# A two-layer transformer trunk on one core: a fifteenth ring slot, and five pieces of work moved on TensorE and VectorE

## The chip, the cores and the metric

The kernel runs on one core of a Trainium2 chip. What is measured is the device time of one execution in microseconds (us); the median over several runs counts.

## What is computed

One sequence of 256 tokens of width 1024 passes two layers, all in float32. Layer 0 mixes tokens with forgetting attention, layer 1 with sparse attention; each is followed by a mixture of 64 experts.

```
for layer in range(2):
    sh_m, sc_m, g_m, sh_f, sc_f, g_f = split(silu(c) @ w_ada[layer] + b_ada[layer], 6)
    u = rmsnorm(h) * (1 + sc_m) + sh_m
    mix = forgetting_attention(u) if layer == 0 else nsa_attention(u, shared_kv(h))
    h = h + g_m * mix
    u = rmsnorm(h) * (1 + sc_f) + sh_f
    h = h + g_f * moe_ffn(u)
# nsa_attention: o = gate0 * o_compressed + gate1 * o_selected + gate2 * o_window
#   o_compressed: softmax of each head's queries over 4 compressed keys, times 4 compressed values
# moe_ffn: s = sigmoid(u @ w_router); the top 8 of 64 by s + bias, weights s / sum * 2.5
#   y = sum over the 8 of weight * (silu(u @ w_eg) * (u @ w_eu)) @ w_ed, plus one shared expert
```

## The kernel before

**The ring.** All large weights pass through `ring` in SBUF, in units of 1 MB. `RING` lists the 484 units in the order in which they are loaded and used; unit n goes to slot n % SLOTS, with SLOTS = 14. The SyncE queue (SP) issues them one after the other (`unit`, `slot_free`): before unit n it waits until TensorE has finished with unit n - SLOTS. There is no other order: if that unit is still held, every later load waits behind it.

**The experts.** In each layer the 64 experts are ordered by how many tokens chose them and cut into 25 groups (`GROUPS`) of one, two or four experts whose rows fill the 128 partitions. An expert has three units: two halves of its gate and up weights, and its down weights. Groups 0 and 1 hold four fixed experts, so that their 12 units can be loaded ahead of the routing. From group 2 on SP must read the order (`order_i`), which routing makes. In `pe_moe` group g runs on TensorE (PE) as: gate and up product (`pe_gate_up`, two halves), gather of the next group's tokens (`pe_gather`, two halves of 8 matmuls), `pe_turn`, the combination of group g - 1 (`combine`), down product (`pe_down`). ScalarE (ACT) copies each gathered half from PSUM (`copy_x`, signalled by `x_ready`). In groups 0 and 1 both halves of a gather are written to the one bank GATHER, so that the second half waits until the first has been copied. `item_tables` makes two small tables in bank Y0 + 1 for experts with more rows than their place holds; before the down product of group 0, which writes that bank, PE waits for `tables_ready`, which VectorE (DVE) gives once it has read them.

**Routing.** At the start of `pe_moe` PE turns the normed rows (`pe_turn_normed`, token tile 0, then tile 1), multiplies by the router weights (`pe_narrow`), turns u back (16 transposes), turns the scores into rows, and then spreads the gate vector over the partitions (`pe_gate`, two matmuls of 128x512 over `gate_diag`, which DVE makes in `dve_gate_diag`). DVE picks the top 8 after it has the scores.

**Sparse attention.** Sixteen batches of four heads (`attention_batches`): 0 to 3 and 8 to 11 are of token tile 0 (128 keys), 4 to 7 and 12 to 15 of tile 1 (256 keys). In step b of `pe_attention` PE makes logits b + 2, weighs values for b - 1 (`weigh`) and turns the probabilities of b (`turn`). In step b of `dve_attention` DVE runs `beside(b)`, masks b + 2 (`mask`) and scales the output of b - 1 (`output`). In step b of `act_attention` ACT takes the exponentials of b and then copies the turned probabilities of b - 1, which `weigh(b - 1)` waits for. Two pieces of DVE work stand beside: at b = 0 the copy of the gates out of bank 6 and `cmp_scores`; at b = 3 `cmp_weights`, five instructions, whose result PE needs first in `weigh(6)` (`CMP_TURNED_AT` is 6).

```
            for b in range(len(batches)):
                if beside:
                    beside(b)
                if b + 2 < len(batches):
                    mask(b + 2)
                if b >= 1:
                    output(b - 1)
```

`add_mix` on DVE then adds the attention's product to h in three pieces of 256 columns, and the last quarter per token tile, each followed by `dve_row_norm`.

## Time and profile before

| | |
|---|---|
| time, median of 3 runs | 1437.22 us (1435.86 to 1437.52) |
| the profiled execution | 1438.07 us, of which the span from first to last instruction is 1436.3 us |
| PE busy | 1381.5 us, 96% of the span |
| DVE, ACT busy | 321.2 us, 266.1 us |
| moved from HBM | 509.89 MB, 356 GB/s over the span |
| share of PE in the chain that ended last | 89% |
| expert groups of layer 0, of layer 1 | about 255 to 731 us, about 953 to 1429 us |

Times in the rows are in us from the start of the span. A matmul's end is modelled, so that a busy PE is not a PE at its peak. A row's bracket gives the idle time of the engine before it and what ended it. PEclk is the clock that TensorE was granted, as a share of 2.4 GHz.

### The profile page before, as it was taken

What the parts mean: (1) busy time and instruction counts of PE and PEld (TensorE: products, weight loads), DVE (VectorE), ACT (ScalarE), POOL (GpSimd) and SP (SyncE); (2) the same over time, 40 slices, a digit from 0 to 9 for tenths busy, and PEclk for the clock granted to TensorE, in tenths of its full rate; (3) what the DMA queues carried; (4) which work ended last, traced back from release to release, by engine and by line L of the source; (5) the groups of instructions that cost most, each with busy time, mean ns of one, the idle gap of its engine ahead of it and who ended that gap; (6) DMA issues with size and microseconds to landing.
All of it is one profiled execution on the core that took longest, in us unless ns stands there. A gap on an engine that the chain in (4) does not pass through costs nothing.

```text
span 1436.3 us, 20547 instructions
## 1 busy us (share of the span) xinstructions
PE 1381.5 (96%) x8361; PEld 788.8 (55%) x8361; DVE 321.2 (22%) x776; ACT 266.1 (19%) x519; POOL 31.6 (2%) x79
## 2 busy tenths in 40 slices
PE   5999899999999999999989988999999999999997
PEld 1777765555644444444458867854564444444442
DVE  1330523111111111111133477231110111111111
ACT  2211523110101111111133365231101111111110
POOL 5000000000100000000000000000010000000000
PEclk9999999999999999999999989999999999999999
DMA  9999289899999999999998600148999999999997
GB/s 376 413 421 421 115 338 407 351 389 420 364 420 421 420 421 420 421 422 420 420 418 332 233 30 1 61 174 363 421 374 404 421 420 421 420 420 421 421 420 289
DMA packets 71599, 512.30 MB, mean 357 GB/s; under 512 B 8240, under 2 KB 8432, under 8 KB 9552
## 3 DMA queue, kind: packets, MB, share of 16 engines
q1 hardware_dynamic: 70560, 509.64, 86.4%
q0 software_dynamic: 800, 1.25, 0.3%
q8 instruction: 68, 1.11, 0.3%
q14 instruction: 27, 0.22, 0.0%
q10 hardware_dynamic: 144, 0.08, 0.0%
HBM read 509.89 MB, written 1.05 MB: 356 GB/s over the span
## 4 chain that ended last, share of the span: by engine, by line
PE 89%; DMA 5%; DVE 3%; ACT 2%; issue 1%; SPq 0%; DVEq 0%; ACTq 0%
PE PS L925 23%; PE PS L915 13%; PE PS L933 12%; PE PS L536 12%; PE PS L949 11%; DMA ring<-in_w_exp 4%; PE PS L563 3%; PE PS L683 2%; PE PS L961 2%; DMA ring<-in_w_ada_units 1%; PE PS L1797 1%; PE PS L515 1%; PE PS L547 1%; PE PS L970 1%; PE PS L666 1%
## 5 line engine op out<-in xcount | busy, mean ns | idle before, releaser
L925 PE MATMUL PS<-ring,scratch 128*32 128x512 f32 (+2 forms) x2176 | 355.4, 597 | 7.3 <-DMA ring<-in_w_exp 5.9
L925 PEld LDWEIGHTS PS<-ring,scratch 128*32 128x32 f32 (+2 forms) x2176 | 111.5, 123 | 244.2 <-issue 242.3
L915 PEld LDWEIGHTS PS<-scratch,u 128*128 128x128 f32 x1600 | 183.0, 192 | 38.7 <-issue 36.8
L915 PE MATMUL PS<-scratch,u 128*128 128x128 f32 x1600 | 192.5, 278 | 1.4 <-ACT scratch L1149 1.4
L933 PE MATMUL PS<-ring,scratch 128*32 128x512 f32 (+2 forms) x1088 | 182.2, 596 | 2.3 <-DVE item_first_i L1265 1.2
L949 PE MATMUL PS<-scratch 128*128 128x512 f32 x384 | 172.7, 592 | 0.0
L1285 DVE TENSOR_TENSOR scratch<-PS,gate_row 128x512 f32<-128x512 f32 x100 | 69.2, 692 | 461.5 <-PE PS L933 461.5
L536 PE MATMUL PS<-ring,uT 128*128 128x256 f32 x672 | 149.3, 381 | 0.4 <-ACT uT L494 0.4
L1157 ACT ACTIVATE scratch<-PS 128x256 f32<-128x256 f32 x50 | 19.2, 384 | 675.2 <-PE PS L925 675.2
L536 PEld LDWEIGHTS PS<-ring,uT 128*128 128x128 f32 x672 | 126.1, 190 | 23.0 <-issue 6.5
L933 PEld LDWEIGHTS PS<-ring,scratch 128*32 128x32 f32 (+2 forms) x1088 | 52.6, 122 | 122.3 <-issue 120.6
L949 PEld LDWEIGHTS PS<-scratch 128*128 128x128 f32 x384 | 69.2, 190 | 68.9 <-issue 68.9
L1273 DVE TENSOR_TENSOR scratch<-scratch,PS 128x256 f32<-128x256 f32 x50 | 21.1, 422 | 331.6 <-ACT scratch L1157 331.6
L1149 ACT ACTIVATE scratch<-PS 128x512 f32<-128x512 f32 x100 | 59.7, 597 | 142.8 <-PE PS L915 142.8
L563 PE MATMUL PS<-ring,cond_cols 128*32 128x512 f32 x448 | 56.5, 626 | 14.3 <-DMA ring<-in_w_ada_units 14.3
L683 PE MATMUL PS<-scratch,uT 128*128 128x65 f32 x288 | 39.2, 289 | 9.7 <-ACT uT L713 9.4
L683 PEld LDWEIGHTS PS<-scratch,uT 128*128 128x128 f32 x288 | 35.9, 201 | 17.0 <-ACT uT L713 15.0
L721 ACT ACTIVATE scratch<-scratch,stats 128x128 f32<-128x128 f32 (+1 forms) x96 | 35.6, 443 | 15.2 <-DVE stats L742 15.2
L563 PEld LDWEIGHTS PS<-ring,cond_cols 128*32 128x32 f32 x448 | 12.1, 111 | 46.5 <-issue 32.4
L1162 ACT ACTIVATE scratch<-PS 128x512 f32<-128x512 f32 x50 | 29.6, 592 | 2.7 <-PE PS L943 2.7
L536 PE MATMUL PS<-ring,u 128*128 128x256 f32 x128 | 28.7, 381 | 0.0
L961 PE MATMUL PS<-uT,ring 128*128 128x256 f32 x128 | 28.3, 379 | 0.0
(332 smaller groups left out, 851.2 us busy)
## 6 DMA issues: line engine op xcount, KB each, us to landing
ring<-in_w_exp SPq DMA_DIRECT2D x384, 1024.0 KB, 16.6
ring<-in_w_ada_units SPq DMA_DIRECT2D x56, 1024.0 KB, 17.0
ring<-in_w_in_a_units SPq DMA_DIRECT2D x12, 1024.0 KB, 26.1
ring<-in_w_cmp_units SPq DMA_DIRECT2D x8, 1024.0 KB, 26.2
ring<-in_w_sh_units SPq DMA_DIRECT2D x6, 1024.0 KB, 13.6
ring<-in_w_kv_b_units SPq DMA_DIRECT2D x6, 1024.0 KB, 22.4
ring<-in_w_o_a_units SPq DMA_DIRECT2D x4, 1024.0 KB, 10.8
ring<-in_w_in_b_units SPq DMA_DIRECT2D x4, 1024.0 KB, 11.3
```

Of the source, the lines that this page charges most:

```text
L536: mm = pe_.matmul(PS[:, bank, t * UC:(t + 1) * UC], lhs[:, k, t * P:(t + 1) * P], w[:, k, :], start=(k == 0), stop=(k == KC - 1))
L563: mm = pe_.matmul(PS[32 * k:32 * k + 32, ADA, :], cond_cols[:, j % 2 * (KC // 2) + k, 31 - r:63 - r], w[:, k, :], start=(j == ada_units(st ...
L683: mm = pe_.matmul(PS[:, heads_bank(kind, b), hd * (DH + 1):(hd + 1) * (DH + 1)], pT[:, n * P:(n + 1) * P], values(br, kt, 4 * g + hd), sta ...
L721: eng.activation(p, p, ACT.Exp, bias=stats[:, b % 3, 4 + i:5 + i]).then_inc(probs_ready, 1)
L915: mm = pe_.matmul(PS[:, bank, i * w:(i + 1) * w], u[:, t, k * P:(k + 1) * P], hot[:, t, :], start=(t == 0), stop=(t == NT - 1))
L925: mm = pe_.matmul(PS[places, GU, :], x[:, kk, places], gate_and_up, start=(kk == 0), stop=(kk == KC - 1))
L933: mm = pe_.matmul(PS[places, Y0 + half, :], hT[:, j, places], down[:, j, half * 512:(half + 1) * 512], start=(j == 0), stop=(j == 1))
L949: mm = pe_.matmul(OUT[t][:, half * 512:(half + 1) * 512], hot_wT[0:rows, t * P:(t + 1) * P], y_rows[0:rows, half * 512:(half + 1) * 512], ...
L961: mm = pe_.matmul(PS[:, GATHER, i * SEQ:(i + 1) * SEQ], slot(AT[unit])[:, k, i * P:(i + 1) * P], uT[:, k, :], start=(k == 0), stop=(k == K ...
L1149: act.activation(x_pair[g % 2][:, 4 * half:4 * half + 4, :].rearrange("p k s -> p (k s)"), PS[:, gather_bank(g, half), :], ACT.Copy).then_ ...
L1162: act.activation(turned_sb[g % 2], PS[:, GU, :], ACT.Copy).then_inc(group_sem["turned_copied"], 1)
L1285: dve.tensor_tensor(y_rows[:, half * 512:(half + 1) * 512], PS[:, Y0 + half, :], gate_row[:, half * 512:(half + 1) * 512], ALU.mult).then_ ...
```

## The change

It has five parts. **Ring:** SLOTS is 15. **Gathers:** the second half of the gather for group 0 goes to bank GU and that for group 1 to bank 0, and PE no longer waits there for the first half's copy; `end_ps` and the item tables move to bank 2, and the wait for `tables_ready` moves from ahead of group 0's down product to ahead of the first `combine` in group 1. **Gates:** DVE copies the gates right after `rotate(3)`, ahead of the first mask, and not after the second. **Compressed weights:** `cmp_weights` runs at b = 6 and not at b = 3. **Last gate:** in layer 1 `gate_diag` is made within `add_mix`, after the second piece; one of its two matmuls stands between the turns of the two token tiles, the other after u has been turned back; and the scores are turned between the two tiles of turning u back.

```
-SLOTS = 14
+SLOTS = 15
...
+        def pe_gate_half(pe_, i, half):
+            return pe_.matmul(PS[:, 4 * (i % 2) + half, :], ones[:, :],
+                              gate_diag[:, 4 * half:4 * half + 4, :].rearrange("p k c -> p (k c)"),
+                              start=True, stop=True)
...
-        def pe_turn_normed(pe_, tag):
+        def pe_turn_normed(pe_, tag, beside_norm=None):
             for t in range(NT):
+                if t == 1 and beside_norm:
+                    beside_norm()
...
-        end_ps = PS[E64, Y0 + 1, 0:1]
+        end_ps = PS[E64, 2, 0:1]
...
         def gather_bank(g, half):
-            return Y0 + 1 if half and g > 1 else GATHER
+            return [GU, 0][g] if half and g <= 1 else Y0 + 1 if half else GATHER
...
-            pe_turn_normed(pe_, tag)
+            def first_of_gate():
+                pe_.wait_ge(gate_diag_ready, 4)
+                pe_.wait_ge(mix_added, 5 * layer + 2)
+                pe_gate_half(pe_, 3, 1)
+
+            pe_turn_normed(pe_, tag, first_of_gate if layer else None)
...
+            turn_back(0)
+            if layer == 0:
+                turn_back(1).then_inc(routing["u_turned"], 1)
             pe_.wait_ge(routing["sigmoids"], layer + 1)
             pe_narrow_rows(pe_, narrow_T[E64, :], scores_ps).then_inc(routing["scores_ready"], 1)
-            pe_gate(pe_, 2 * layer + 1)
+            if layer == 0:
+                pe_gate(pe_, 1)
+            else:
+                turn_back(1).then_inc(routing["u_turned"], 1)
+                pe_gate_half(pe_, 3, 0).then_inc(gate_out, 1)
...
-            pe_.wait_ge(*by_group("x_ready", layer, 1))
-            pe_gather(pe_, one_hot[0], range(4, 8)).then_inc(group_sem["gathered"], 1)
+            pe_gather(pe_, one_hot[0], range(4, 8), gather_bank(0, 1)).then_inc(group_sem["gathered"], 1)
...
                     if g:
                         pe_.wait_ge(*by_group("y_ready", layer, 2 * g))
-                    else:
-                        pe_.wait_ge(*by_group("x_ready", layer, 3))
...
                 if g:
+                    if g == 1:
+                        pe_.wait_ge(routing["tables_ready"], layer + 1)
                     combine(g - 1)
                 else:
                     item_tables()
-                    pe_.wait_ge(routing["tables_ready"], layer + 1)
...
-            dve_gate_diag(done, 2 * layer + 1)
+            if layer == 0:
+                dve_gate_diag(done, 1)
...
+                    if (layer, j) == (1, 1):
+                        dve.wait_ge(gate_out, 3)
+                        dve_gate_diag(done, 3)
...
             rotate(3)
+            dve.wait_ge(sem("gates_turned"), 1)
+            done(dve.tensor_copy(gates[:, :, :], narrow_rows(6, SEQ, 3 * H)), sem("gates_ready"))
...
                 if b == 0:
-                    dve.wait_ge(sem("gates_turned"), 1)
-                    done(dve.tensor_copy(gates[:, :, :], narrow_rows(6, SEQ, 3 * H)), sem("gates_ready"))
                     cmp_scores()
-                elif b == 3:
+                elif b == CMP_TURNED_AT:
                     cmp_weights()
```

On PE, where layer 1's expert part begins, before the change (L547 is the last quarter of the attention's output product, L827 the turn of the normed rows, L515 the router product, L994 turning u back, L523 turning the scores, L605 the gate):

```order
L547 MATMUL PS<-ring,uT 128x256 x16
L827 MATMUL PS<-ident,u 128x128 x16
L515 MATMUL PS<-uT,scratch 64x256 x8
L994 MATMUL PS<-ident,uT 128x128 x16
L523 MATMUL PS<-ident,narrow_T 128x64 x2
L605 MATMUL PS<-scratch,ones 128x512 x2
L1003 MATMUL PS<-scratch,before 128x64
```

The same place after the change (L831, L1006 and L608 are the former L827, L994 and L605):

```order
L547 MATMUL PS<-ring,uT 128x256 x16
L831 MATMUL PS<-ident,u 128x128 x8
L608 MATMUL PS<-scratch,ones 128x512
L831 MATMUL PS<-ident,u 128x128 x8
L515 MATMUL PS<-uT,scratch 64x256 x8
L1006 MATMUL PS<-ident,uT 128x128 x8
L523 MATMUL PS<-ident,narrow_T 128x64 x2
L1006 MATMUL PS<-ident,uT 128x128 x8
L608 MATMUL PS<-scratch,ones 128x512
L1023 MATMUL PS<-scratch,before 128x64
```

One gate matmul has moved between the two turns, and 8 transposes from ahead of the scores to behind them.

On DVE, in the sparse attention before the change, between output 1 (L2215) and mask 5 (L738, L741, L742) stand the five instructions of `cmp_weights`:

```order
L2215 TENSOR_TENSOR u<-PS,stats 128x256
L2191 TENSOR_REDUCE small<-scratch 128x32
L2192 RECIPROCAL small<-small 128x32
L2193 TENSOR_TENSOR small<-small,gates 128x32
L2195 TENSOR_TENSOR scratch<-scratch 128x128
L2196 TENSOR_TENSOR scratch<-scratch,small 128x128
L738 TENSOR_TENSOR scratch<-PS,causal 128x1024
```

After the change they stand between output 4 (L2237) and mask 8 (L740), the first of the second branch:

```order
L2237 TENSOR_TENSOR u<-PS,stats 128x256
L2215 TENSOR_REDUCE small<-scratch 128x32
L2216 RECIPROCAL small<-small 128x32
L2217 TENSOR_TENSOR small<-small,gates 128x32
L2219 TENSOR_TENSOR scratch<-scratch 128x128
L2220 TENSOR_TENSOR scratch<-scratch,small 128x128
L740 TENSOR_TENSOR scratch<-PS,causal 128x512
```

So three masks of 256 keys (5, 6 and 7) now run ahead of them, and the mask behind them is one of 128 keys.

On DVE in `add_mix` of layer 1 after the change (L841, L843 are a piece's product and sum, L2102, L2104 those of the last quarter), `gate_diag` (L597) has moved from behind the modulation to between the second and the third piece:

```order
L841 TENSOR_TENSOR scratch<-PS,gate_row 128x512
L843 TENSOR_TENSOR h<-h,scratch 128x2x256
L597 TENSOR_TENSOR scratch<-ident,vectors 128x1024
L841 TENSOR_TENSOR scratch<-PS,gate_row 128x512
L843 TENSOR_TENSOR h<-h,scratch 128x2x256
L2102 TENSOR_TENSOR scratch<-PS,gate_row 128x256
L2104 TENSOR_TENSOR h<-h,scratch 128x256
```

## Rows read from the trace of the kernel before

**Rows 1.** Busy time by stretch, most of each layer's expert groups; last columns PEclk, DMA, GB/s.

```profile
390.00:714.00 324.00, 323.82 (x1936) 152.16 (x1934) 43.60 (x90) 35.13 (x68) 0.00 (x0) 1.00 1.01 421
1090.00:1412.00 322.00, 321.78 (x1931) 151.35 (x1929) 43.61 (x90) 35.13 (x68) 0.00 (x0) 1.00 1.01 421
```

**Rows 2.** PE's waits over the whole span: total, times, longest.

```profile
PE PS L925 <- DMA ring<-in_w_exp: 5.9, 2, 3.2
```

**Rows 3.** PE's timeline, last group of layer 0: second gate/up half, down product.

```profile
716.59 5.34 PE L925 MATMUL PS<-ring,scratch 128*32 128x512 f32 x32 [2.77 <-DMA ring<-in_w_exp]
...
727.04 2.35 PE L933 MATMUL PS<-ring,scratch 128*32 128x512 f32 x20
```

**Rows 4.** The same of layer 1.

```profile
1414.94 3.64 PE L925 MATMUL PS<-ring,scratch 128*32 128x512 f32 x32 [3.17 <-DMA ring<-in_w_exp]
...
1424.85 3.64 PE L933 MATMUL PS<-ring,scratch 128*32 128x512 f32 x32 [1.09 <-DMA ring<-in_w_exp]
```

**Rows 5.** The chain that ended last: start, length of its two long transfers.

```profile
692.85 23.61 DMA ring<-in_w_exp
...
1397.81 26.90 DMA ring<-in_w_exp
```

**Rows 6.** What the DMA engines moved from 1066 to 1086 us, slices of 0.5 us.

```profile
GB/s 442 410 410 475 377 426 426 164 98 66 49 0 147 98 197 426 377 492 328 262 66 213 328 475 426 360 164 147 164 344 442 475 328 377 262 328 410 459 328 410
```

**Rows 7.** Timelines of PE and ACT, layer 0, end of group 0.

```profile
265.38 2.05 PE L915 MATMUL PS<-scratch,u 128*128 128x128 f32 x16 [0.69 <-ACT scratch L1149]
...
268.80 3.65 PE L933 MATMUL PS<-ring,scratch 128*64 128x512 f32 x16 [0.62 <-DVE item_first_i L1265]
...
267.96 0.59 ACT L1162 ACTIVATE scratch<-PS 128x512 f32<-128x512 f32 x1
```

**Rows 8.** Timelines in the sparse attention, batches 3 to 6: DVE, ACT, PE.

```profile
847.08 0.29 DVE L2191 TENSOR_REDUCE small<-scratch 128x32 f32<-128x128 f32 x1
...
848.35 0.29 DVE L2196 TENSOR_TENSOR scratch<-scratch,small 128x128 f32<-128x128 f32 x1
...
851.40 1.71 ACT L721 ACTIVATE scratch<-scratch,stats 128x256 f32<-128x256 f32 x4 [3.01 <-DVE stats L742]
...
854.06 3.67 PE L683 MATMUL PS<-scratch,uT 128*128 128x65 f32 x16 [2.57 <-ACT uT L713]
...
860.55 2.00 PE L683 MATMUL PS<-scratch,uT 128*128 128x65 f32 x16
...
864.55 2.00 PE L683 MATMUL PS<-scratch,uT 128*128 128x65 f32 x16 [0.47 <-ACT uT L713]
```

**Rows 9.** Busy time by stretch: PE, weight loads, DVE, ACT, POOL; PEclk third last.

```profile
848.64:872.05 23.41, 19.76 (x152) 17.55 (x151) 17.68 (x39) 12.13 (x27) 0.00 (x0) 0.85 0.01 1
935.00:939.00 4.00, 3.97 (x11) 2.24 (x12) 2.32 (x4) 2.35 (x4) 0.00 (x0) 0.57 0.00 0
853.50:860.50 7.00, 6.39 (x32) 5.87 (x32) 5.55 (x11) 3.24 (x7) 0.00 (x0) 0.52 0.00 0
```

**Rows 10.** Timelines of PE and ACT where the gates are awaited.

```profile
836.42 1.05 PE L1744 MATMUL PS<-own_group,ada_parts 128*128 128x32 f32 x8 [1.32 <-DVE gates L2202]
...
835.57 0.58 ACT L1953 ACTIVATE ada_parts<-PS 128x512 f32<-128x512 f32 x1
```

**Rows 11.** PE's timeline into layer 1's routing; then the router product of layer 0.

```profile
933.59 1.09 PE L827 MATMUL PS<-ident,u 128*128 128x128 f32 x8 [1.82 <-DVE u L818]
935.03 5.35 PE L515 MATMUL PS<-uT,scratch 128*64 128x256 f32 x16 [0.35 <-DMA scratch<-in_w_router_rows]
940.32 1.97 PE L994 MATMUL PS<-ident,uT 128*128 128x128 f32 x16
...
237.91 3.64 PE L515 MATMUL PS<-uT,scratch 128*64 128x256 f32 x16 [0.15 <-ACT uT L494]
```

**Rows 12.** DVE's timeline there: third piece of the mix, and the gate's diagonal.

```profile
924.10 0.69 DVE L837 TENSOR_TENSOR scratch<-PS,gate_row 128x512 f32<-128x512 f32 x1 [2.94 <-PE PS L1797]
...
936.11 1.22 DVE L597 TENSOR_TENSOR scratch<-ident,vectors 128x1024 f32<-128x1024 f32 x1
```

More of the change, by code:

```diff
@@ L603, in pe_gate @@
             pe_.wait_ge(gate_diag_ready, i + 1)
-            for half in range(2):
-                mm = pe_.matmul(PS[:, 4 * (i % 2) + half, :], ones[:, :],
-                                gate_diag[:, 4 * half:4 * half + 4, :].rearrange("p k c -> p (k c)"),
-                                start=True, stop=True)
-            mm.then_inc(gate_out, 1)
+            pe_gate_half(pe_, i, 0)
+            pe_gate_half(pe_, i, 1).then_inc(gate_out, 1)
+        def pe_gate_half(pe_, i, half):
+            return pe_.matmul(PS[:, 4 * (i % 2) + half, :], ones[:, :],
+                              gate_diag[:, 4 * half:4 * half + 4, :].rearrange("p k c -> p (k c)"),
+                              start=True, stop=True)
         def act_gate(done, i):
@@ L899, in build @@
         count_ranked_ps = PS[E64, Y0, 320:321]
-        end_ps = PS[E64, Y0 + 1, 0:1]
-        n_items_ps = PS[0:1, Y0 + 1, 1:2]
-        item_rank_ps = PS[0:1, Y0 + 1, 128:128 + MAX_ITEMS]
-        item_base_ps = PS[0:1, Y0 + 1, 192:192 + MAX_ITEMS]
+        end_ps = PS[E64, 2, 0:1]
+        n_items_ps = PS[0:1, 2, 1:2]
+        item_rank_ps = PS[0:1, 2, 128:128 + MAX_ITEMS]
+        item_base_ps = PS[0:1, 2, 192:192 + MAX_ITEMS]
         count_col, rank_col, key_e, n_over, end_col, begin_col, base_col = (e_cols[E64, i:i + 1] for i in range(7))
         def gather_bank(g, half):
-            return Y0 + 1 if half and g > 1 else GATHER
+            return [GU, 0][g] if half and g <= 1 else Y0 + 1 if half else GATHER
         def pe_gather(pe_, hot, chunks, bank=GATHER):
@@ L989, in pe_moe, with turn_back @@
                 pe_ada_columns(pe_, 2)
-            for t in range(NT):
+            def turn_back(t):
                 for k in range(KC):
@@ L995, in pe_moe @@
                                        uT[:, k, t * P:(t + 1) * P], ident[:, :])
-            mm.then_inc(routing["u_turned"], 1)
+                return mm
+            turn_back(0)
+            if layer == 0:
+                turn_back(1).then_inc(routing["u_turned"], 1)
             pe_.wait_ge(routing["sigmoids"], layer + 1)
             pe_narrow_rows(pe_, narrow_T[E64, :], scores_ps).then_inc(routing["scores_ready"], 1)
-            pe_gate(pe_, 2 * layer + 1)
+            if layer == 0:
[3 more added lines that the diff above has]
+                pe_gate_half(pe_, 3, 0).then_inc(gate_out, 1)
             pe_.wait_ge(routing["mask_ready"], layer + 1)
```

## The prediction

> **What bounds the kernel now.** I read the busy time by stretch first, then PE's waits, then the timelines where it waits. Through most of the expert groups both bounds are at work at once: PE is busy without a gap and the DMA engines move 421 GB/s [rows 1]. One unit is 1.049 MB, so it takes 2.49 us at that rate. PE hardly waits for weights: twice, 5.9 us together [rows 2], and both waits stand in the last group of a layer [rows 3, 4]. So PE sets the pace from group 0 on, the loads lose a little ground to it, and at the end of each layer the loads have become the bound. The chain that ended last shows the same: it goes through PE and then through one transfer, from 692.85 to 716.46 in layer 0 and from 1397.81 to 1424.71 in layer 1 [rows 5]. Those transfers are long because they stand in a full queue, not because they are slow.
>
> What ties the loads' end is the last time at which the ring was full and the DMA engines stood idle. That is at about 1069.5 to 1080 us: the rate falls from above 400 to between 0 and 200 GB/s three times [rows 6], since SP may issue only as PE frees a slot. Behind it the rate is 421 GB/s to the end [rows 1]. So each layer's loads end at that event, which PE times, plus the number of units still to come.
>
> Ahead of the experts of layer 1 PE waits for DVE and ACT instead: in the attention [rows 8, 10] and at the router [rows 11]. An idle spell there can cost twice, as the granted clock falls behind it: 0.52 from 853.5 to 860.5 and 0.57 from 935 to 939 [rows 9], the lower of the two levels (1.2 GHz) for nearly all of the stretch.
>
> **The change part by part.**
>
> *Ring.* With 15 slots SP is one unit further when the ring is last full, and all behind it come 2.49 us earlier, in each layer. In layer 1 PE waits 3.17 us for the second gate/up half and 1.09 us for the down weights [rows 4]. Both waits depend on loads that come 2.49 us earlier, and PE's own work between them is unchanged, so 0.68 us is left of the first and the second stays: **2.49 us** gained. In layer 0 more is to be had. PE's second half starts at 716.59 after 2.77 us, and takes 5.34 us, where the same 32 matmuls took 3.64 in layer 1 [rows 3, 4]: the clock had fallen behind the wait. With 0.28 us of it left I take the full clock. In layer 1 PE was ready for the down product 8.82 us after that half's start (1424.85 - 1.09 - 1414.94) [rows 4]; in layer 0 that would be 714.10 + 8.82 = 722.9. The last down unit landed at 716.46 + 4 x 2.49 = 726.4 [rows 5] and now lands at 723.9, so the loads decide, and the down product starts at 724.0 in place of 727.04 [rows 3]: **3.0 us**. If PE has slack nowhere else, this needs no other change. Its bounds are 0 (the loads don't get ahead) and the whole waits, 2.77 + 1.7 and 3.17 + 1.09.
>
> *Gathers and tables.* In group 0, PE waited 0.69 us between the halves of the gather and 0.62 us for the tables [rows 7]. The first wait goes whole: nothing else is behind it. The second doesn't: ACT's copy of what `pe_turn` made ended at 268.55 [rows 7], 0.25 us before the down product started, and PE needs that copy too. It moves with the gather, so I take 0.69 + 0.2 = **0.9 us in each layer**, 1.8 in all; 1.4 without the second part, 2.6 if both waits went whole. Both move PE, and as PE times the last full ring, the loads come as much earlier. Moving the tables' wait ahead of `combine` costs nothing: a down product and a whole gate/up product of work (3.65 us for the first alone [rows 7]) lie between. The same change for group 0's own gather costs and gives nothing, since small products stand between its halves. The wait for the last copy of group 0's tokens stays.
>
> *Gates.* PE waited 1.32 us, and the row names DVE's gates [rows 10]. But the same matmuls also read `ada_parts`, whose copy by ACT ended at 836.15 [rows 10], only 0.27 before. So 0.1 us, 0.3 at most. On DVE the copy stands in another place with the same length ahead of the second mask's end.
>
> *Compressed weights.* The five instructions run from 847.08 to 848.64, 1.6 us [rows 8]. Behind them comes mask 5, then the exponentials of batch 5 at 851.40 (ACT had waited 3.01 us for them), and only behind these ACT's copy for `weigh(4)`, which PE reaches at 854.06 after 2.57 us [rows 8]. With the five away, and the 0.1 from above, `weigh(4)` starts 1.7 us earlier, at 852.4, and 0.9 us of the wait is left. Then there is the clock. From this `weigh` to the next PE took 6.49 us (854.06 to 860.55), at 0.52 of the clock; the next such step, at full clock, took 4.00 [rows 8, 9]. With 0.9 us of idle time in place of 2.57, I take the clock as kept: 2.49 us more. Sum **4.2 us**. DVE must be able to follow. From 848.64 to 872.05, where it begins to be the bound again, it was busy for 17.68 of 23.41 us in 39 instructions [rows 9]; each is followed by a pause of 0.03 us (848.64 to 848.68 behind the last of the five is one), 1.2 in all, so 4.5 us was waiting. Adding the moved 1.6, it needs 20.5 where 25.0 went by: it can come 4.5 earlier, and so follows the 4.2. The result is needed in `weigh(6)`, at 852.4 + 2 x 4.0 = 860.4; the five end on DVE once mask 7 and output 4 are done, about 859.3, by the order of its work. If the clock falls all the same, 1.7 us remains; if DVE merely waits elsewhere, 0.
>
> *Last gate.* Making the diagonal takes 1.22 us and now stands ahead of the third piece, where DVE sat idle for 2.94 us [rows 12]: no cost; without that cover it would be 1.2. One gate matmul of 512 columns fills part of the 1.82 us before the second turn. Its length is at least 0.5 us, a quarter of the 2048 columns that were turned in 1.97 us [rows 11], and I take twice that, as a product of two full f32 operands should cost more per column than a turn; at either end it fits into the wait and delays nothing. What it may give is the clock: the router product took 5.35 us in layer 1 and 3.64 in layer 0, where PE was busy until it [rows 11], so **1.7 us**, or 0. Turning back half of u behind the scores takes half of 1.97 us [rows 11] off the way to DVE's top 8: 0.95 us. From there DVE's chain leads to the first gather without waiting; ACT's copy of u ends as late as before, and its gate copy comes 0.1 to 0.2 earlier, just not in the way. I take **0.9 us**, 0.5 if ACT comes last.
>
> **The clock's rule.** The trace shows two drops behind waits of 1.82 and 2.57 us [rows 9, 8, 11], and none behind the longest, 3.17 us, since the product behind it took 3.64 us [rows 4]. The Trainium skill, "TensorE: Matmul & The Clock Gate", Part 1, explains it: the window in which activity is judged runs freely, and the place of a drop can vary with the phase. By that, shifting the program may take a drop away here and set one there. The trace agrees as far as a long wait without a drop goes; the rule gives weight to rival 1.
>
> **Sum.** 2.49 + 3.0 + 1.8 + 4.2 + 1.7 + 0.9 = 14.1 us. Span 1436.3 - 14.1 = 1422.2; the profiled run of 1438.07 becomes 1424.0, and the median of 1437.22, 0.85 less than that run, **1423.1 us**.
>
> **Rivals.**
> 1. *The clock falls elsewhere or still* (one or two of: batch 4, the router, or a place that kept it so far). Each costs 1.7 to 2.5 us (5.35 - 3.64; 6.49 - 4.00) [rows 8, 11]. For it: idle spells stay at every one of these places, and the whole of layer 1 is shifted. Against: the spells are a half to a third as long. 1425 to 1428 us.
> 2. *The wait moves within the attention.* DVE has but 0.3 us to spare over PE, and mask 8 now stands behind the five instructions. If they only delay it instead of mask 5, 4.2 shrinks to 1.7 or nothing: 1425.6 to 1427.3 us. Against: 4.5 us of waiting in that stretch [rows 9].
> 3. *The ring's slot gives nothing*, as if the queue of issued transfers and not the slots held the loads back, or PE were slower by another wait: 14.1 - 5.5 = 8.6, 1428.6 us. Against it are the idle DMA engines [rows 6].
> 4. *Slower than before.* Each transfer behind the last full ring takes longer, because the deeper ring is served less evenly. About 130 units per layer follow (324 / 2.49) [rows 1]. An interval longer by 14.1 / 260 = 0.054 us, 2.2%, takes everything back, and at 4% the time is 1436 + 12 = 1449 us. Nothing in the trace bears on it: the rate is 421 GB/s however full the queue is [rows 1].
>
> **Chances and range.** The forecast (1421.3 to 1424.9) 0.53; rival 1 0.27; rival 2 0.07; rival 3 0.07; rival 4 0.02; better than forecast, if a drop that I left in place goes too, 0.04. The range reaches from 1420.8 to 1428.2. A measurement of this kernel can tell about 0.2%, 2.9 us, from no change; only rival 4 and a pile of the others fall short of that. Faster 0.96, same 0.02, slower 0.02.
>
> **What would show it.** *Ring:* the wait at the last group's second half falls to about 0.3 us in layer 0 and 0.7 in layer 1; that in front of the last down product stays near 1.1 us. *Group 0:* the waits of 0.69 and 0.62 us are replaced by one of some 0.4 us. *Attention:* a wait of about 0.9 us before `weigh(4)`, PEclk 1.00 behind it, and 4.2 us less between mask 4 and mask 11. *Router:* the product takes 3.6 us, and the wait ahead of the second turn is 0.8 to 1.3 us. Wrong would be: PEclk near 0.5 in a new place (rival 1), no wait left in a layer's last group while the layer is not 2.5 us shorter (PE is the bound, rival 3), or a rate below 421 GB/s (rival 4).

## The result and the profile after

The kernel after takes 1433.12 us (median of 20 runs, 1428.43 to 1438.13) beside 1438.34 us of the kernel before in the same series (20 runs, 1435.52 to 1450.51): a ratio of 0.9944, 95% interval 0.9925 to 0.9962. It is faster, by 5 us where 14 were forecast, and lies above the range. The profiled execution took 1437.93 us, its span is 1436.2 us, and its mean granted clock 0.983. Two executions stand apart, one of 5055.77 us in e6 and one of 1819.46 us of the kernel before beside it, and count in no median here.

I cut each trace at four starts of TensorE (PE) rows: the first gate/up product of layer 0, the last down product of layer 0, the first logits of the sparse attention, and the first turn of normed rows ahead of layer 1's router; then the same two rows of layer 1. The lengths between them, in us:

| | start to experts 0 | experts 0 | to first logits | sparse attention and mix | router to experts 1 | experts 1 | span |
|---|---|---|---|---|---|---|---|
| before | 255.31 | 471.73 | 102.71 | 100.99 | 22.53 | 471.59 | 1436.3 |
| after | 260.51 | 467.80 | 103.57 | 105.30 | 19.91 | 467.63 | 1436.2 |
| after, second trace | 255.05 | 467.30 | 102.71 | 105.30 | 19.96 | 468.40 | 1430.3 |

Three stretches got shorter, as forecast. Three got longer: the start and, by 0.9 us behind a fall of the clock at 739.7, the way to the first logits, both in this execution only; and the sparse attention, where 4.2 us less were forecast and 4.3 more came.

The waits at each layer's end in the timeline of after (the rows that answer to [rows 3, 4]):

```profile
714.29 3.64 PE L930 MATMUL PS<-ring,scratch 128*32 128x512 f32 x32
718.21 3.64 PE L930 MATMUL PS<-ring,scratch 128*32 128x512 f32 x32 [0.29 <-DMA ring<-in_w_exp]
...
728.31 3.64 PE L938 MATMUL PS<-ring,scratch 128*32 128x512 f32 x32 [1.29 <-DMA ring<-in_w_exp]
...
1414.85 3.64 PE L930 MATMUL PS<-ring,scratch 128*32 128x512 f32 x32 [0.34 <-DMA ring<-in_w_exp]
...
1424.73 3.64 PE L938 MATMUL PS<-ring,scratch 128*32 128x512 f32 x32 [1.07 <-DMA ring<-in_w_exp]
```

The waits for the second gate/up half, 2.77 and 3.17 us before, are 0.29 and 0.34, and layer 0's half runs at full clock (3.64 us, not 5.34). Between them the busy time by stretch shows what it did in [rows 1], PE without a gap and 421 GB/s:

```profile
390.00:714.00 324.00, 324.00 (x1926) 154.13 (x1925) 42.57 (x88) 36.62 (x71) 0.00 (x0) 1.00 1.01 421
1090.00:1410.00 320.00, 320.00 (x1903) 151.48 (x1903) 42.57 (x88) 35.13 (x68) 0.00 (x0) 1.00 1.01 421
```

Group 0, where [rows 7] had waits of 0.69 and 0.62 us: the gather is one run of 32 matmuls, and what is left is 0.47 us ahead of the down product. From group 0's first gate/up product to group 1's it is 15.85 us, before 16.98.

```profile
260.51 7.09 PE L930 MATMUL PS<-ring,scratch 128*64 128x512 f32 x32 [0.69 <-ACT scratch L1167]
...
267.85 3.84 PE L920 MATMUL PS<-scratch,u 128*128 128x128 f32 x32
...
272.91 3.65 PE L938 MATMUL PS<-ring,scratch 128*64 128x512 f32 x16 [0.47 <-issue]
```

`weigh(4)` of the sparse attention, the gates' product and the router, which answer to [rows 8, 10, 11]:

```profile
838.34 1.08 PE L1763 MATMUL PS<-own_group,ada_parts 128*128 128x32 f32 x8 [1.10 <-ACT ada_parts L1972]
...
853.97 2.00 PE L685 MATMUL PS<-scratch,uT 128*128 128x65 f32 x16 [0.96 <-ACT uT L715]
...
940.05 1.10 PE L831 MATMUL PS<-ident,u 128*128 128x128 f32 x8 [0.96 <-DVE u L820]
941.46 3.67 PE L515 MATMUL PS<-uT,scratch 128*64 128x256 f32 x16 [0.32 <-DMA scratch<-in_w_router_rows]
```

The wait of 2.57 us is 0.96, and the step behind it takes 2.00 us, full clock; the gates' product now waits for ACT, as the second releaser was. All of this the prediction had. What it had not stands 28 us further on, in the timeline from the first batch over 256 keys of the second branch, `weigh(12)`:

```profile
881.87 2.59 PE L685 MATMUL PS<-scratch,uT 128*128 128x65 f32 x16 [1.43 <-ACT uT L715]
884.26 1.91 PE L668 MATMUL PS<-ident,scratch 128*128 128x128 f32 x8
887.29 3.67 PE L685 MATMUL PS<-scratch,uT 128*128 128x65 f32 x16 [1.11 <-ACT uT L715]
...
892.60 3.78 PE L1786 MATMUL PS<-scratch 32*128 32x128 f32 x32
896.31 3.68 PE L685 MATMUL PS<-scratch,uT 128*128 128x65 f32 x16
```

The same steps in the kernel before, with the same wait:

```profile
884.48 2.00 PE L683 MATMUL PS<-scratch,uT 128*128 128x65 f32 x16 [1.43 <-ACT uT L713]
886.31 1.04 PE L666 MATMUL PS<-ident,scratch 128*128 128x128 f32 x8
888.53 1.66 PE L683 MATMUL PS<-scratch,uT 128*128 128x65 f32 x13 [1.17 <-ACT uT L713]
```

16 matmuls of 128x65 take 3.67 us in place of 2.00, eight turns 1.91 in place of 1.04. The busy time by stretch of after names it (behind the stretch's length PE's busy us; PEclk third last); the other three rows are falls in its start:

```profile
883.00:904.00 21.00, 19.89 (x110) 18.93 (x110) 7.59 (x21) 7.05 (x12) 0.00 (x0) 0.51 0.00 1
16.00:23.00 7.00, 5.86 (x26) 2.46 (x27) 0.00 (x0) 0.00 (x0) 0.84 (x4) 0.51 1.01 421
29.00:37.00 8.00, 6.79 (x20) 2.45 (x19) 2.24 (x6) 1.94 (x4) 6.78 (x13) 0.57 1.00 343
176.00:187.00 11.00, 9.89 (x49) 7.49 (x48) 1.21 (x4) 2.05 (x2) 0.00 (x0) 0.53 0.01 1
```

The same stretch in before:

```profile
883.00:904.00 21.00, 18.39 (x163) 17.42 (x162) 12.55 (x28) 8.76 (x16) 0.00 (x0) 1.00 0.00 1
```

For about 20.5 us TensorE is granted the lower of its two levels (1.2 GHz), though it is busy in 19.89 of 21.00 us. By the slices of 1 us, before's falls in the attention were of 3.4 and 6.8 us. I call the one of 20.5 us the long fall. The start of this execution has three falls (6.8, 6.8 and 10.2 us) where before has one of 3.4 us, and took 5.2 us longer.

### The profile page after: what moved, and what is told of

It is laid out like the page before. It is cut to its first block, busy times and chain, and to the rows that moved or that the text cites. A ratio compares the mean times of both kernels' runs of the same rounds, so it can differ in the third digit from the quotient of the medians.

```text
span 1436.2 us, 20550 instructions
## 1 busy us (share of the span) xinstructions
PE 1390.0 (97%) x8361; PEld 799.3 (56%) x8361; DVE 321.2 (22%) x776; ACT 266.7 (19%) x519; POOL 31.5 (2%) x79
## 4 chain that ended last, share of the span: by engine, by line
PE 89%; DMA 5%; DVE 3%; ACT 2%; issue 1%; SPq 0%; DVEq 0%; ACTq 0%
PE PS L930 23%; PE PS L920 13%; PE PS L938 12%; PE PS L536 12%; PE PS L954 11%; DMA ring<-in_w_exp 3%; PE PS L563 3%; PE PS L685 2%; PE PS L966 2%; DMA ring<-in_w_ada_units 1%; PE PS L1816 1%; PE PS L515 1%; PE PS L668 1%; PE PS L547 1%; PE PS L975 1%
## 5 line engine op out<-in xcount | busy, mean ns | idle before, releaser
L685 PE MATMUL PS<-scratch,uT 128*128 128x65 f32 x288 | 43.0, 307 | 9.1 <-ACT uT L715 9.1
L685 PEld LDWEIGHTS PS<-scratch,uT 128*128 128x128 f32 x288 | 39.6, 218 | 17.6 <-ACT uT L715 16.0
L723 ACT ACTIVATE scratch<-scratch,stats 128x128 f32<-128x128 f32 (+1 forms) x96 | 35.6, 443 | 13.8 <-DVE stats L744 13.7
```

What stands on the lines that cost most here:

```text
L685: mm = pe_.matmul(PS[:, heads_bank(kind, b), hd * (DH + 1):(hd + 1) * (DH + 1)], pT[:, n * P:(n + 1) * P], values(br, kt, 4 * g + hd), sta ...
L723: eng.activation(p, p, ACT.Exp, bias=stats[:, b % 3, 4 + i:5 + i]).then_inc(probs_ready, 1)
```

## The experiments

The theory: all terms of the sum came in, and what is missing went into the clock, above all into the long fall, which idle time of PE ahead of `weigh(12)` sets off. Rivals: the long fall is chance, a property of one execution; or what is missing went into a wait or into slower transfers. All kernels that have "fill" in their name add products whose results go to PSUM columns that nothing reads; they leave nothing out. "Attention" below is the fourth column of the table above, and a fall's length is the sum over slices of 1 us of what is missing from full clock, doubled.

**Is it chance? Both kernels traced again.** No edit: the kernel before once, the kernel after three times.

> The kernel before, unchanged, as a second look. Theory A (both kernels lose TensorE's clock for a while at some of their idle spells, and which ones differs from run to run; the profile before was a mild draw): the stretches of lowered clock stand at other places than 716, 840, 854 and 935 us in part, the spans differ by 2 us or more between runs and go with the clock (longer at a lower mean clock), and at an equal mean clock this kernel is 8 to 14 us longer than the changed one. Theory B (the change itself brings longer drops, above all the one of 20 us at 882 to 903): this kernel shows no stretch of more than 8 us at the lowered clock in any look, and its mean clock stays at 0.990 to 0.994.

> The changed kernel, unchanged, as a second look. Theory A: the drops from 176 to 188 and from 882 to 903 are not both there again; from the first gate/up product of layer 0 to the last down product of layer 0 it takes 467.8 us again, and the same of layer 1 467.6, as these stretches hold no drop. Theory B: a drop of about 20 us in the second half of the sparse attention is there again, and the stretch from layer 0's end to layer 1's first gate/up product takes about 219 us again.

> The changed kernel again, unchanged, for the place of its long drop. If the code sets it: a drop of about 20 us begins 50 to 52 us after the attention's first logits once more, and the stretch takes 105.3 us. If only the phase of the run sets it: the drop is absent or stands elsewhere and the stretch takes 96.5 to 101 us.

> The changed kernel once more, same question as in its third look: 105.3 us and a drop 50 to 52 us behind the first logits if the code sets it, 96.5 to 101 us if the phase does.

| | attention | long fall | median, runs | ratio, interval |
|---|---|---|---|---|
| before again | 100.62 | none | 1441.65, 12 | 1.0015, 0.9989 to 1.0042 |
| after, second | 105.30 | 876 to 898 | 1432.62, 12 | 0.9942, 0.9917 to 0.9968 |
| after, third | 105.29 | 877 to 898 | 1432.83, 9 | 0.9934, 0.9899 to 0.9969 |
| after, fourth | 105.29 | 878 to 899 | 1432.70, 10 | 0.9941, 0.9912 to 0.9969 |

Hardly chance: it is there in four traces of four, at the same step, and the attention agrees to 0.01 us. Each trace is of one execution; of the others only the time and the mean clock are known. A fall of 20.5 us takes 10.2 us of 1430 from the clock, so that a run with it has a mean of 0.993 at most, by my estimate. Of after's 51 runs 49 have 0.992 or less. Two, of 1429.40 us (0.994) and 1422.97 us (0.996), can't have had the long fall, so the program doesn't bring it every time. For the kernel before the means say little, since other falls take as much. The start does vary by chance: 255.05, 255.20 and 256.06 us in these traces of after, 260.51 in the first. The row of the second trace shows the fall:

```profile
876.00:898.00 22.00, 20.89 (x120) 19.93 (x119) 7.77 (x21) 7.08 (x12) 0.00 (x0) 0.53 0.00 1
```

The trace of before gave something else. Its router product ran at full clock without any change:

```profile
933.16 1.09 PE L827 MATMUL PS<-ident,u 128*128 128x128 f32 x8 [1.82 <-DVE u L818]
934.60 3.67 PE L515 MATMUL PS<-uT,scratch 128*64 128x256 f32 x16 [0.35 <-DMA scratch<-in_w_router_rows]
```

The stretch from router to experts is 20.84 us there, 22.53 in the first profile. So the 1.7 us that I read off [rows 11] belonged to that execution, and only the 0.9 of the routing order is sure to be the change's. Of the seven traces with the old order here, three have such a fall (22.47 to 22.54 us) and four have none (20.79 to 20.90); in the 13 with the new order the stretch is 19.82 to 20.02 us.

**One part at a time.** The ring alone in the kernel before (e4), the compressed weights alone (e6, and again e11), and all of the change without the compressed weights (e5):

```
-SLOTS = 14
+SLOTS = 15
```

```
-                elif b == 3:
+                elif b == CMP_TURNED_AT:
```

> The kernel before with SLOTS = 15 and nothing else. The ring's term as I reckoned it: the wait at the last group's second gate/up half falls from 2.8 to 3.2 us to 0.3 to 0.7, the wait before the last down product stays near 1.1, and from the first gate/up product to the last down product each layer is 2.5 us (layer 1) to 3.0 us (layer 0) shorter than before (471.7 and 471.6 us). Rival, the slot gives nothing: the waits and both stretches stay within 0.3 us.

> The kernel before with the compressed weights at step 6, nothing else. If the move brings the long drop: it stands in the second half of the attention here too, and the stretch takes about 105 us, 4 more than before; median 2 to 5 us above the kernel before. If my sum were right as it stood: the stretch takes 96.5 us and the median falls by 4.

> The kernel before with the compressed weights at step 6, again. Its first look had no drop behind the first batches and took 96.9 us. If the phase decides: this look may show the long drop and 104 to 106 us, or none again; if the other parts of the change are needed for the long drop: none again, 96.9 us.

> The changed kernel with the compressed weights back at step 3, nothing else. If the move is what brings the drop of 20 us in the second half of the sparse attention: no drop there, one of about 7 us before the first 256-key batch's values as in the kernel before, the stretch from the attention's first logits to the turn of the rows for layer 1's experts near 100.7 us again and not 105.3, and the whole 3 to 5 us shorter than the changed kernel. If the drop comes with the other parts or by chance: the stretch stays near 105 us or goes to 109.

| | experts 0 | experts 1 | attention | long fall | median, runs | ratio, interval |
|---|---|---|---|---|---|---|
| before, 15 slots (e4) | 469.07 | 468.75 | 100.70 | none | 1434.12, 12 | 0.9948, 0.9919 to 0.9977 |
| before, weights at 6 (e6) | 471.62 | 471.72 | 96.89 | none | 1437.88, 11 | 1.0000, 0.9971 to 1.0029 |
| the same again (e11) | 471.56 | 471.82 | 97.82 | none | 1441.32, 10 | 0.9988, 0.9955 to 1.0021 |
| after, weights at 3 (e5) | 467.37 | 467.60 | 100.51 | none | 1428.97, 12 | 0.9949, 0.9921 to 0.9978 |

The ring takes 2.66 and 2.84 us from the layers, 5.50 together (forecast 5.49); what the whole change takes beyond it, 1.27 and 1.12, is the gathers' (forecast 0.9 each). In other traces of after this rest is 1.4 to 1.8 and 0.4 to 1.1; group 0 alone gives it more sharply, as the way from its gate/up product to group 1's is 16.97 to 16.98 us in every trace without this part and 15.85 in every trace with it, 1.12 us less in each layer. The compressed weights take 4.1 us from the attention (100.99 to 96.89; forecast 4.2) in e6 and 3.2 in e11. So each term is there, and no wait took one back. But the medians of e6 and e11 are those of before (0.9971 to 1.0029, 0.9955 to 1.0021), and e6's trace is of one of its fastest runs: what the other runs lose again isn't traced. The long fall is in none of the four; e4 has one of 13.7 us in the first eight batches. In e5 the old wait is back, and the clock falls behind it as before, a short time:

```profile
849.73 3.58 PE L685 MATMUL PS<-scratch,uT 128*128 128x65 f32 x16 [2.56 <-ACT uT L715]
853.11 1.91 PE L668 MATMUL PS<-ident,scratch 128*128 128x128 f32 x8
```

**Which parts together bring it?** The gates' copy moved back in after (e13); in before, weights at 6 and the gates early (e14); in before, weights at 6 and 15 slots (e16); after with SLOTS at 14 (e17).

```
             rotate(3)
-            dve.wait_ge(sem("gates_turned"), 1)
-            done(dve.tensor_copy(gates[:, :, :], narrow_rows(6, SEQ, 3 * H)), sem("gates_ready"))
...
                 if b == 0:
+                    dve.wait_ge(sem("gates_turned"), 1)
+                    done(dve.tensor_copy(gates[:, :, :], narrow_rows(6, SEQ, 3 * H)), sem("gates_ready"))
                     cmp_scores()
```

> The changed kernel with the gates' copy back behind the second mask, nothing else. Theory C (the long drop comes where no short drop stands in the first eight batches, and the gates' move is what takes the short one away): a drop of 3 to 7 us about 9 us behind the first logits, none in the second half, the stretch of the attention 96.9 to 97.8 us instead of 105.3, median 6 to 8 us below the changed kernel, about 1426. If the long drop needs only the compressed weights' move and another part (ring, gathers, last gate): it stays, 105.3 us and 1432.5.

> The kernel before with the compressed weights at step 6 and the gates' copy with the last rotation, nothing else. Theory C: no drop in the first eight batches, one of about 20 us from 51 us behind the first logits, 105 us for the stretch, so 8 us more than with the compressed weights' move alone. Otherwise 96.9 to 97.8 us, as there.

> The kernel before with the two parts that took the most time out together: fifteen units and the compressed keys and values turned behind the seventh mask (CMP_TURNED_AT 6 in place of 3). Neither part alone had the 20.5-us stretch at half clock. If the two together bring it (the last group's wait of 2.77 us and the compressed logits' wait of 2.57 us are both gone, so that TensorE comes to the second branch's first wait of 1.43 us, 50 us behind the first logits, without an earlier fall), it stands about 50 us behind the first logits and the attention from its first logits to the ffn's turning takes 105 us. If gathers, the gates or the last gate are needed for it, the stretch is absent and the attention takes 97 to 98 us. Median by the first theory about 1431 to 1434, by the second 1425 to 1430.

> The kernel after with SLOTS back at 14, all else as changed. The last group of each layer should lose its 2.5 to 3.5 us again (layers of about 471.0 and 471.3 in place of 467.7). By the theory that the fifteenth unit takes part in the long stretch at half clock, the stretch is absent and the attention takes 97 to 98 us: median about 1431 to 1434. By the theory that it comes from the edits within the attention alone, it stays: attention 105 us, median about 1437.

| | attention | falls in it (length) | median, runs | ratio, interval |
|---|---|---|---|---|
| after, gates late (e13) | 105.48 | 876 to 898 (20.5) | 1431.30, 12 | 0.9927, 0.9901 to 0.9953 |
| before, weights at 6, gates early (e14) | 100.69 | 838 to 853 (13.7) | 1438.30, 12 | 0.9973, 0.9940 to 1.0005 |
| before, weights at 6, 15 slots (e16) | 103.14 | 836 to 847 (10.2), 880 to 891 (10.2) | 1435.24, 10 | 0.9959, 0.9919 to 1.0000 |
| after, 14 slots (e17) | 97.83 | 836 to 844 (6.8) | 1437.44, 10 | 0.9978, 0.9943 to 1.0013 |

The gates' copy isn't needed for it (e13), and doesn't bring it together with the weights (e14), where an earlier fall of 13.7 us takes back what the weights gave. e16 shows a fall at the same `weigh(12)`, half as long, and e17 none; e17's layers take 470.09 and 471.13 us, so it has lost the ring's term again, as expected. The timeline of e16, then of e17:

```profile
879.74 2.97 PE L683 MATMUL PS<-scratch,uT 128*128 128x65 f32 x16 [1.42 <-ACT uT L713]
882.50 1.91 PE L666 MATMUL PS<-ident,scratch 128*128 128x128 f32 x8
885.53 3.67 PE L683 MATMUL PS<-scratch,uT 128*128 128x65 f32 x16 [1.11 <-ACT uT L713]
```

```profile
880.70 2.00 PE L685 MATMUL PS<-scratch,uT 128*128 128x65 f32 x16 [1.43 <-ACT uT L715]
882.53 1.04 PE L668 MATMUL PS<-ident,scratch 128*128 128x128 f32 x8
884.75 2.00 PE L685 MATMUL PS<-scratch,uT 128*128 128x65 f32 x16 [1.17 <-ACT uT L715]
```

The busy time by stretch of e16, then of e17:

```profile
878.00:892.00 14.00, 11.46 (x72) 10.41 (x70) 9.20 (x19) 7.03 (x13) 0.00 (x0) 0.63 0.00 1
```

```profile
878.00:898.00 20.00, 17.40 (x157) 16.04 (x156) 13.03 (x32) 9.94 (x18) 0.00 (x0) 1.00 0.01 2
```

The waits are the same to 0.06 us; in one the clock falls behind them, in the other not. Over all traces: kernels with both 15 slots and the weights at 6, and the wait as it is, fell there in 6 of 6; kernels with at most one of the two in 0 of 8. The step `weigh(12)` starts between 875 and 882 us in e16, e17, e6 (880.15) and the traces of after, so that its place in time doesn't tell them apart. Nor does PE's work just before: from `weigh(4)` to `weigh(12)` it is 27.89 to 27.91 us in all six that fell and in e4, e6, e11, e14 and e17, which didn't.

What does tell them apart is where the step stands between two moments at which the clock may change. In each of the 20 traces all changes of the granted clock stand on one grid of equal steps, to 0.003 us. A slice of 1 us places a change: here, of after, it is at 883.1, and of e17 at 836.5.

```profile
883.00:884.00 1.00, 1.00 (x7) 1.00 (x7) 0.86 (x5) 0.74 (x2) 0.00 (x0) 0.55 0.00 0
```

```profile
836.00:837.00 1.00, 0.72 (x7) 0.61 (x6) 0.19 (x1) 1.00 (x4) 0.00 (x0) 0.74 0.00 0
```

The start of `weigh(12)`, as a share of the way from one grid moment to the next:

| wait as it is | share | fall there |
|---|---|---|
| after, four traces | 0.64, 0.52, 0.51, 0.54 | yes |
| e13, e16 | 0.67, 0.76 | yes |
| before, e1 | 0.12, 0.98 | no |
| e4, e5, e6 | 0.10, 0.92, 0.93 | no |
| e11, e14, e17 | 0.96, 0.13, 0.95 | no |

All six that fell lie between 0.51 and 0.76, all eight that didn't between 0.92 and 1.13. The two parts shift the step along this grid, as any part would that changes the time ahead of it.

**Fill the waits.** Three products of 128x120 are issued on PE ahead of its wait for the turned probabilities, in `weigh`, and this wait moves behind the one for the bank. Shown is e18; in e3 and e7 only the condition differs, and e8, e9 and e15 have a helper for the products, one in place of three at some batches, and more places.

```
-                pe_.wait_ge(probsT_ready, b0 + b + 1)
                 if b >= 2:
                     pe_.wait_ge(heads_read, b0 + b - 1)
...
+                if kind == "nsa" and b == 12:
+                    for _ in range(3):
+                        pe_.matmul(PS[:, heads_bank(kind, b), 264:384], ident[:, :], causal[:, 0:120],
+                                   start=True, stop=True)
+                pe_.wait_ge(probsT_ready, b0 + b + 1)
```

e3 fills every batch over 256 keys of both attentions but one; e7 the last four batches of the sparse one; e18 `weigh(12)` alone. e8 fills nearly every wait of the kernel that isn't at a layer's end, the ones between the first units too; e9 leaves these out and has one product ahead of batches 0 to 3; e15 leaves out also those at the start of layer 1 and ahead of the sparse attention's batches below 8.

> The changed kernel, with three extra products of 128x120 into unused columns of the bank ahead of each wait for turned probabilities of a 256-key batch, in both attentions (nothing of the result is touched). Theory A, that the clock falls because of the idle spells in the attention: no drop in either attention, sparse attention at full clock throughout, so 5 to 10 us less than the changed kernel's median and less spread, 1424 to 1428 us. If idle spells of under 1.5 us have nothing to do with it: the drops stay, and the time is that of the changed kernel or up to 2 us more.

> The changed kernel with three extra products ahead of the waits of the last four batches of the sparse attention only. If the long drop starts from the idle spells of these batches (0.4, 1.4 and 1.1 us): it is gone, the stretch takes 96.5 to 97.5 us, and the median is 6 to 8 us below the changed kernel's, about 1425. If it starts from what goes before them: it stays, 105 us.

> The changed kernel with extra products in every larger wait of TensorE outside the expert groups: one ahead of each 256-key batch of the first branch, three in the other 256-key batches of both attentions, two before the last rotated queries and the compressed logits, five and two around the turn at the start of layer 1, two after each of the first units, five ahead of the forget product. If idle spells set the drops: mean clock 0.998 or more in nearly all runs, spread of the spans under 2 us, median 1421 to 1424. If drops come by themselves: mean clock and spread as in the run with fewer products (0.989 to 0.999, 7 us).

> As the run with products in all larger waits, but without those between the first units (they made the start 4 us longer), with one more ahead of each of the first four batches of the sparse attention and three instead of two before the last rotated queries and the compressed logits. If idle spells set the drops: no drop from 150 us on, mean clock 0.998 or more, the start back at 255 us, the stretch of the sparse attention 97 to 98.5 us, median 1423 to 1426 and below every other version. If what is left of drops comes by itself: mean clock as in the run before, median about 1429.

> The changed kernel with three extra products ahead of the waits in the 256-key batches of the first attention and in the last four of the sparse attention, three ahead of the forget product, of the last rotated queries and of the compressed logits, and none at the start of layer 1 (there they delayed the turn by 1.4 us) or in the sparse attention's first half. If idle spells set the drops: no drop from 150 us on in most runs, mean clock 0.995 to 0.999, attention 97 to 98 us, median 1423 to 1426, the fastest version of all.

> The kernel after with three products of 120 columns (written to columns that nothing reads) ahead of one wait alone, that of the first batch over 256 keys of the second attention, 1.43 us long, where the 20.5-us stretch began in four of four looks; the wait of 1.11 us behind it stays. If that one wait brings the stretch, it is gone, the attention takes 97 to 98 us and the median is about 1427, as with all four waits filled. If the waits count together, the stretch comes later or shorter, and the attention takes 99 to 105 us, median 1429 to 1433.

| | start to experts 0 | attention | falls in it (length) | span | median, runs | ratio, interval |
|---|---|---|---|---|---|---|
| e3 | 254.31 | 101.35 | 834 to 845 (10.2) | 1425.0 | 1429.82, 11 | 0.9923, 0.9897 to 0.9949 |
| e7 | 255.38 | 97.84 | none | 1422.5 | 1427.16, 7 | 0.9917, 0.9884 to 0.9950 |
| e8 | 259.59 | 99.29 | 837 to 845 (6.8) | 1429.8 | 1433.43, 12 | 0.9945, 0.9918 to 0.9971 |
| e9 | 254.14 | 97.52 | none | 1425.1 | 1426.33, 6 | 0.9883, 0.9843 to 0.9924 |
| e15 | 254.17 | 102.28 | 834 to 848 (13.7) | 1425.7 | 1427.09, 6 | 0.9904, 0.9880 to 0.9928 |
| e18 | 255.30 | 96.56 | none | 1421.3 | 1424.13, 10 | 0.9902, 0.9870 to 0.9933 |

The long fall is gone in 6 of 6. On the grid above e3, e9 and e15 have `weigh(12)` at 0.01, 0.27 and 0.23, where it might have stayed away anyhow. e7 and e18, at 0.58 and 0.68, stand where all unfilled ones fell, and e8 at 0.82 just beyond. e18 is the sharpest: one wait filled, 1.43 us down to 0.51, and the next, 1.27 us and untouched, sets nothing off. Its timeline and its busy time by stretch:

```profile
874.42 0.93 PE L682 MATMUL PS<-causal,ident 128*128 128x120 f32 x6
875.86 2.00 PE L689 MATMUL PS<-scratch,uT 128*128 128x65 f32 x16 [0.51 <-ACT uT L719]
877.69 1.04 PE L668 MATMUL PS<-ident,scratch 128*128 128x128 f32 x8
880.00 1.97 PE L689 MATMUL PS<-scratch,uT 128*128 128x65 f32 x16 [1.27 <-ACT uT L719]
```

```profile
876.00:898.00 22.00, 20.73 (x176) 19.64 (x177) 10.99 (x26) 8.54 (x15) 0.00 (x0) 1.00 0.00 1
```

The attention takes 96.56 us in place of 105.30, and the median is 8.5 to 9.0 us below the four of after. Eight of its ten runs took 1423.06 to 1425.49 us, below the lowest of the 20 runs of after, with mean clocks of 0.994 to 0.999, so that they can't hold the long fall; of after's 51 runs two are such. The other two, of 1432.44 and 1432.82 us at 0.987 and 0.988, lost clock somewhere that isn't traced. It has the lowest median of all, with one edit of three products; by the ratio to before it can't be told from e9 (0.9843 to 0.9924). More products weren't better. Those of e8 between the first units lie on the path: experts 0 start 5.45 us later than in e9, which leaves them out. e8 was expected at 1421 to 1424 us and took 1433.43; e15 was expected to be the fastest, and wasn't. In e3, e8 and e15 the clock falls in the first eight batches, for 6.8 to 13.7 us, though e3 and e8 fill waits there too.

## Why the prediction was wrong

**Right: every wait.** Against before, by stretches: the ring 5.50 us (forecast 5.49), the gathers 2.4 (1.8; 2.2 by group 0's own rows), the compressed weights 4.1 (4.2, in e6), the router 2.6 (2.6). The ring's mechanism held in detail: the waits for the second gate/up half fell to 0.29 and 0.34 us (forecast 0.3 and 0.7), those ahead of the last down product are 1.29 and 1.07 (forecast about 1.1). Split by layer the ring's term is less exact: in layer 0 the ring alone gave 2.66 (forecast 3.0), in layer 1 2.84 (forecast 2.49). The wait at `weigh(4)` is 0.96 us (forecast 0.9), at the second turn 0.96 (0.8 to 1.3), and the clock behind `weigh(4)` is 1.00. In e18 all of it is in one execution and nothing is lost: span 1421.3 us where the sum gave 1422.2, median 1424.13 where it gave 1423.1.

**Wrong: the step on the clock.** The prediction says "With 0.9 us of idle time in place of 2.57, I take the clock as kept". At that step it was. But the sum then took the clock everywhere else to stay as it was in the one profile of before, and I never considered `weigh(12)`: a wait of 1.43 us, without a fall in before, has one of 20.5 us behind it in each trace of after. So the failed step is this: falls behind waits that the change leaves alone stand in the sum with nothing. Rival 1 had the mechanism ("a place that kept it so far", chance 0.27), but its size was off by a factor of three to five: I priced a fall by the two short ones of the profile, 1.7 to 2.5 us, and this one costs 8.7 us (105.30 - 96.56). That is about the whole miss: 14.1 - 8.7 = 5.4 us, and the medians differ by 5.2.

**Half wrong: a gain that was luck.** Of the 2.6 us at the router 1.7 came from a fall that the kernel before doesn't always have (e1). A term that rests on a fall read in one profile is worth its chance times its size. The paragraph on the clock's rule also counts too few: before's trace has, besides the two drops named there, the one behind the 2.77 us of [rows 3] and one of 3.4 us at 839.7, in the attention, which nothing in the sum takes up.

**Rivals 2 to 4** fell: no wait took the place of the one removed (e6), the slot gave its 5.50 us (e4), and the rate is 421 GB/s with either depth.

**The page's rule, measured.** The starts of the traces vary from run to run by falls that come and go: 255.05 to 260.51 us in four traces of after, with the same program. The Trainium skill, "TensorE: Matmul & The Clock Gate", Part 1, states that the window runs freely and that the same kernel's cold spell varies; the trace agrees there. The long fall stood at one step in all four traces all the same: from the end of the start's last fall `weigh(12)` comes 841.40 to 841.52 us later in the second to fourth trace of after, so the step meets nearly the same place of the grid each time. The same part states that sustained activity releases the throttle; here PE was busy, as the profile models it, 19.89 of 21.00 us and was held at the lower level throughout, so busy time alone didn't release it.

**What stays open.** That the wait ahead of `weigh(12)` sets the long fall off is shown by e18, with e7 beside it: they stand where all six unfilled traces fell, and didn't fall. Why it does so only with both the fifteenth slot and the late weights is argued, not shown. The step's place on the grid of clock changes sorts all 14 unfilled traces, and PE's work for 28 us before it is the same in both groups; by that the two parts matter only through the time that they take away, and another part of the right length would do it too. No run shifted the step without one of the parts (a plain pause ahead of the attention would), each kernel but after has one or two traces, and the rule was read from the traces that it sorts. What PE did earlier isn't ruled out either; e16, which had a fall before and still fell at `weigh(12)`, speaks against its simplest form, that an earlier fall prevents the later one. Also not settled is why the fall lasts 20.5 us in after and 10.2 in e16.

## What to carry to other kernels

Before adding up waits, list every idle spell of TensorE over a microsecond in stretches where it works in small products, also those behind which the clock is full today: taking away time elsewhere shifts them, and can bring a fall behind one of them. Here it ate 8.7 of 14 us. Price a fall by more than one profile, and where a wait can't be removed, small products ahead of it can keep the clock, and three cost nothing here; put them at the one wait that sets the fall off, and trace it again, since others may only move it. A part measured alone (the compressed weights, ratio 1.0000) can be worth 4 us in its stretch of one trace and nothing in the median, so read both, and trace more than one run.

## What the runs showed of the hardware

- A fall of the clock can last 20.5 us with TensorE 95% busy (19.89 of 21.00 us), behind a wait of 1.43 us. Other falls took 3.4, 6.8, 10.2 and 13.7 us; in that of 13.7 us in e4 TensorE was busy for 14.00 of 14.00 us (842 to 856).
- Within a trace the changes of the granted clock stand on one grid of equal steps, to 0.003 us in all 20 traces.
- The kernel before, run again unchanged beside itself, gave medians of 1441.65 and 1437.40 us. Its single runs go from 1435.3 to 1451.0 us, with mean granted clocks of 0.990 to 0.994 below 1437 us, but for a few at 0.989, and of 0.979 above 1450 us. No trace is of such a long run, so where they lose the clock isn't known. As the two medians are 4.25 us apart, differences under that between medians of ten or twelve runs say little here, and the stretches of a trace say more.
- In the kernel before the fall at the router came in the first trace and was absent in the second, with the same wait of 1.82 us ahead of it.
